# Decay sums of a gated delta rule: turned and spread by rounded products; the query norm folded into the output norm

## The reference, cut to what matters

```python
q = l2_normalize(q) * HEAD_DK ** -0.5          # after convolution and silu
k = l2_normalize(k)
g = jnp.cumsum(g_chunk)                        # log decay; exp(g_i - g_j) for j <= i
a_mat = strict * (k_beta @ k.T) * decay        # triangular system of a chunk, inverted
qk = lower * (q @ k.T) * decay
q_dec = q * jnp.exp(g)                         # meets the state: o = q_dec @ S + qk @ v_new
...
o = rms_norm_2(o_fwd + o_bwd, out_norm_g) * silu(z)
```

## Time and profile before

| | us |
|---|---|
| median of 3 runs | 1171.09 |
| lowest and highest run | 1166.39, 1172.75 |
| profiled execution: span from first to last instruction | 1167.6 |
| TensorE busy | 1019.9 (87%) |
| VectorE busy | 506.4 (43%) |
| ScalarE busy | 380.4 (33%) |
| GpSimd busy | 427.5 (37%) |

### The profile page before, as it was taken

The page is one execution under the profiler, slowest core; times in us unless marked ns, Lnnn a source line. Parts: engine busy times, 40 slices in busy tenths (PEclk is TensorE's granted clock), DMA queues, the critical chain, the costliest instruction groups (busy, mean ns, idle before and its releaser), DMA issues.

```text
span 1167.6 us, 20205 instructions
## 1 busy us (share of the span) xinstructions
PE 1019.9 (87%) x8173; PEld 802.9 (69%) x8173; DVE 506.4 (43%) x980; ACT 380.4 (33%) x572; POOL 427.5 (37%) x192
## 2 busy tenths in 40 slices
PE   8999999999999999999999899966767667666685
PEld 6999999999999999797989797423323232332231
DVE  4346965601136887767854543222222222222213
ACT  5554354444447656334343344100000000000002
POOL 6767868888876866143031281000000000000000
PEclk9999999999999999999999899988888888888898
DMA  7644546566656544215220889999999999999995
GB/s 248 219 129 146 178 129 187 175 192 186 183 178 196 165 146 137 59 37 217 93 80 12 326 293 383 388 425 428 429 427 428 429 427 429 428 428 429 428 420 202
DMA packets 43569, 304.75 MB, mean 261 GB/s; under 512 B 5092, under 2 KB 5476, under 8 KB 30952
## 3 DMA queue, kind: packets, MB, share of 16 engines
q1 hardware_dynamic: 43208, 303.21, 69.1%
q10 hardware_dynamic: 288, 0.52, 0.1%
HBM read 302.67 MB, written 1.05 MB: 260 GB/s over the span
## 4 chain that ended last, share of the span: by engine, by line
PE 57%; DMA 27%; DVE 8%; POOL 2%; issue 2%; ACT 2%; SPq 2%; DVEq 0%; ACTq 0%; POOLq 0%
DMA arena<-gate_up 24%; PE bank L484 11%; PE bank L485 11%; PE bank L486 10%; PE bank L1357 6%; PE bank L862 5%; PE bank L1378 3%; POOL rounded L2966 1%; DMA weights<-front 1%; DMA arena<-down 1%; PE bank L826 1%; DVE arena L2091 1%; POOL rounded L2925 1%; SPq L3010 1%; PE bank L1097 1%
## 5 line engine op out<-in xcount | busy, mean ns | idle before, releaser
L2925 POOL TENSOR_TENSOR rounded<-weights,rounded 128x1024 fp32r<-128x1024 f32 x152 | 370.4, 2463 | 156.3 <-ACT rounded L1443 146.9
L484 PE MATMUL bank<-rounded 128*128 128x256 f32 (+2 forms) x776 | 219.2, 282 | 2.2 <-POOL rounded L2925 2.2
L485 PE MATMUL bank<-rounded 128*128 128x256 f32 (+2 forms) x776 | 216.5, 279 | 0.0
L486 PE MATMUL bank<-rounded 128*128 128x256 f32 (+2 forms) x776 | 216.2, 279 | 0.0
L1443 ACT ACTIVATE rounded<-weights 128x1024 fp32r<-128x1024 f32 x146 | 147.4, 1052 | 80.6 <-PE bank L486 47.6
L484 PE MATMUL bank<-rounded,rounded 128*128 128x256 f32 (+3 forms) x552 | 158.3, 287 | 2.1 <-DVEq L2346 0.8
L485 PE MATMUL bank<-rounded,rounded 128*128 128x256 f32 (+3 forms) x552 | 156.2, 283 | 0.0
L486 PE MATMUL bank<-rounded,rounded 128*128 128x256 f32 (+3 forms) x552 | 156.1, 283 | 0.0
L484 PEld LDWEIGHTS bank<-rounded 128*128 128x128 f32 (+1 forms) x776 | 145.6, 188 | 4.3 <-POOL rounded L2925 2.9
L485 PEld LDWEIGHTS bank<-rounded 128*128 128x128 f32 (+1 forms) x776 | 145.5, 187 | 0.7 <-issue 0.6
L486 PEld LDWEIGHTS bank<-rounded 128*128 128x128 f32 (+1 forms) x776 | 145.2, 187 | 0.0
(11 more groups left out here) (465 smaller groups left out, 1456.6 us busy)
## 6 DMA issues: line engine op xcount, KB each, us to landing
weights<-front SPq DMA_DIRECT2D x165, 512.0 KB, 4.2
arena<-down SPq DMA_DIRECT2D x31, 2048.0 KB, 22.0
weights<-gate_up SPq DMA_DIRECT2D x28, 2048.0 KB, 34.7
arena<-gate_up SPq DMA_DIRECT2D x28, 2048.0 KB, 33.4
weights<-front SPq DMA_DIRECT2D x4, 2048.0 KB, 8.0
weights<-gate_up SPq DMA_DIRECT2D x8, 768.0 KB, 12.5
arena<-gate_up SPq DMA_DIRECT2D x4, 1536.0 KB, 33.7
weights<-gate_up SPq DMA_DIRECT2D x4, 512.0 KB, 7.3
```

What stands on the lines that cost most here:

```text
L484: nc.tensor.matmul(out, a[0], b[1], start=start, stop=False)
L485: nc.tensor.matmul(out, a[0], b[0], start=False, stop=False)
L486: return nc.tensor.matmul(out, a[1], b[0], start=False, stop=stop)
L2925: nc.gpsimd.tensor_tensor(lo, raw[q % RAW], hi.bitcast(f32), ALU.subtract).then_inc(sem("w_lo"), 1)
```

## The change

A unit is now two heads and both tiles. The decay sums of all heads are no longer formed by a product for each head: TensorE transposes the running sums `gsum` once (turn_rows), VectorE copies them as a rounded part and a rest (rows_r, partitions 0 to 15 and 32 to 47), and one rounded product of 48 rows with a picking column spreads a head's row of 256 tokens over all partitions. ScalarE makes the query exponentials from the same banks, directly after the exponentials of the unit, and it hands the banks back instead of VectorE. The decay sums in query_unit, the query factors, their spreading and the normalization of q are gone: as o is linear in q, the squared norm of q goes into the epsilon of the output norm (q_sums). `qd` and `inv` move to the end of the arena, where down weights arrive later; so two loads change places in SyncE's queue. `pairs` is formed between the convolutions of q0 and q1, GpSimd clears `inv` before its last four weight halves, and the substitution and query products are interleaved anew.

The diff, cut to its core (indentation reduced, unchanged lines left out):

```diff
@@ -290,12 +290,14 @@
 rn2_r = rounded(RING + top[0], LEN)
+q_sums = arena[:, top[0]:top[0] + SEQ]
...
-inv = place(32 * 32).rearrange("p (i j) -> p i j", i=32)
+inv_home = ARENA - BLOCK + 24 * P
+inv = arena[:, inv_home:inv_home + 32 * 32].rearrange("p (i j) -> p i j", i=32)
@@ -312,7 +314,11 @@
-qd = ring[2].rearrange("p (s c) -> p s c", s=LH)
+late_home = ARENA - BLOCK
+qd = arena[:, late_home:late_home + 24 * P].rearrange("p (s c) -> p s c", s=24)
+rows_r = rounded(RING + k_tok_at, 2 * P)
+pick_row_r = rounded(RING + k_tok_at + 2 * P, 16)
+ROW_SPREAD = 48
@@ -348,6 +354,14 @@
+def pair_lanes(x, d, u):
...
+    return x[:, 16 * d:16 * d + 16, :].rearrange("p (t h) c -> p t h c", t=TT)[:, :, 2 * u:2 * u + 2, :]
...
+def pair_of(bank):
...
+    return bank[:, :].rearrange("p (i t c) -> p t i c", i=2, t=TT)
@@ -967,21 +982,31 @@
             end(f, last)
...
+    def turn_rows():
...
+        f = begin("rows")
+        pe.wait_ge(sem("gl"), 4)
+        for t in range(TT):
+            last = nc.tensor.transpose(f.bank[0:16, t * P:(t + 1) * P], gsum[:, t + 1, 0:16], ident)
+        end(f, last)
...
-        tile, half = UNITS[u]
-        at = META + (tile - 1) * P
+        pe.wait_ge(sem("gl"), 5)
+        pe.wait_ge(sem("edec"), 1)
...
-            for h in range(4):
-                j = i * HEADS + 4 * half + h
-                last = nc.tensor.matmul(f.bank[:, h * P:(h + 1) * P], gl[:, tile, j:j + 1].to_broadcast([P, P]), omask(m),
+            for h in range(2):
+                j = i * HEADS + 2 * u + h
+                last = nc.tensor.matmul(f.bank[:, h * SEQ:(h + 1) * SEQ],
+                                        pick_row_r[0:ROW_SPREAD, j:j + 1].to_broadcast([ROW_SPREAD, P]), rows_r[0:ROW_SPREAD],
...
-        for h in range(4):
-            k = kT[:, 4 * half + h, at:at + P]
-            last = nc.tensor.matmul(f.bank[:, h * P:(h + 1) * P], k, k, start=True, stop=True)
+        for h in range(2):
+            for t in range(TT):
+                k = kT[:, 2 * u + h, META + t * P:META + (t + 1) * P]
+                last = nc.tensor.matmul(f.bank[:, (2 * h + t) * P:(2 * h + t + 1) * P], k, k, start=True, stop=True)
@@ -993,13 +1018,6 @@
         end(f, last)
-        for d, i, m in DIRS[0:1 if tile == TT else 2]:
-            f = begin(f"grow_{d}{u}")
-            for h in range(4):
-                j = i * HEADS + 4 * half + h
-                last = nc.tensor.matmul(f.bank[:, h * P:(h + 1) * P], gl[:, tile, j:j + 1].to_broadcast([P, P]), omask(m),
-                                        start=True, stop=True)
-            end(f, last)
@@ -1113,12 +1131,12 @@
     norms("nk", sq_k, LEN, ("sqn", 1, 2))
-    turn[WK] += 1
+    turn_rows()
...
@@ -1156,23 +1174,16 @@
     norms("nq", sq_q, SEQ, ("sqn", 3, 4))
+    query_unit(0)
...
+    query_unit(1)
...
-    spread("q", 0, 2, SEQ)
+    query_unit(2)
...
-    spread("q", 1, 2, SEQ)
-    turn[WK] += 1
-    z_part(4)
-    pe.wait_ge(sem("q_done"), 2)
-    query_unit(0)
-    z_part(5)
-    query_unit(1)
-    z_part(6)
-    query_unit(2)
-    z_part(7)
...
+    for n in range(4, 8): z_part(n)
@@ -1629,6 +1640,10 @@
         act.sem_inc(sem("gate_f"), 1)
...
+    act.wait_ge(sem("gl"), 1)
+    for a in (0, 32):
+        last = nc.scalar.activation(pick_row_r[a:a + 16, :], ident[a:a + 16, a:a + 16], ACT.Copy)
+    link(last)
@@ -1693,16 +1708,15 @@
             act.wait_ge(sem("unit_u"), 2 * u + i + 1)
-            e = qk[:, unit_lanes(i, u), :]
+            e = pair_lanes(qk, i, u)
...
-    def query_exps(u):
...
-        tile, half = UNITS[u]
-        for d, i, m in DIRS[0:1 if tile == TT else 2]:
-            f = got(f"grow_{d}{u}")
-            link(nc.scalar.activation(qd[:, unit_lanes(i, u), :], four_of(f.bank), ACT.Exp))
+        for d, i, m in DIRS:
+            f = fills[f"row_{d}{u}"]
+            if d == "f":
+                link(nc.scalar.activation(pair_lanes(qd, 0, u), pair_of(f.bank), ACT.Exp))
+            else:
+                link(nc.scalar.activation(qd[:, 16 + 2 * u:16 + 2 * u + 2, :], pair_of(f.bank)[:, 0], ACT.Exp))
@@ -1759,7 +1773,6 @@
     silu_sq("q", 1, qT[:, 4:8], SEQ, sq_q[:, 4:8])
-    norm_sqrt("nq", SEQ, ("ssn", 3), "sdn")
@@ -1767,11 +1780,7 @@
     take_gate("zz", 1)
-    query_exps(0)
-    query_exps(1)
...
-    query_exps(2)
-    query_exps(3)
@@ -2346,11 +2355,14 @@
         dve.sem_inc(sem(f"conv_{kind}"), 1)
...
-    def factors(name, n, rows_r, scale, signal, root, count):
+    def factors(name, n, rows_r, signal, root, count, of_queries=None):
...
-        link(nc.vector.tensor_scalar(rn, rn, scale, EPS, ALU.mult, ALU.add))
+        if of_queries is None:
+            link(nc.vector.tensor_scalar(rn, rn, 1.0, EPS, ALU.mult, ALU.add))
+        else:
+            link(nc.vector.scalar_tensor_tensor(rn, rn, 1.0 / P, of_queries, ALU.mult, ALU.add))
@@ -2367,6 +2379,8 @@
     link(nc.vector.memset(rn2_r.bitcast(f32), 0.0))
+    nc.vector.memset(rows_r.bitcast(f32), 0.0)
+    nc.vector.memset(pick_row_r.bitcast(f32), 0.0).then_inc(sem("gl"), 1)
@@ -2422,9 +2436,14 @@
         conv(f"v{h}", v_T[0][:, h, :], "v", 16 + h)
-    factors("nk", LEN, rn2_r, 1.0, "ssn", "sdn", 1)
+    factors("nk", LEN, rn2_r, "ssn", "sdn", 1)
...
+    f = got("rows")
+    link(nc.vector.tensor_copy(rows_r[0:16], f.bank[0:16, 0:SEQ]))
+    link(nc.vector.tensor_tensor(rows_r[32:48], f.bank[0:16, 0:SEQ], rows_r[0:16].bitcast(f32), ALU.subtract))
+    dve.sem_inc(free[f.b], 1)
+    dve.sem_inc(sem("gl"), 1)
@@ -2494,29 +2513,29 @@
     def unit_rows(u):
...
-        tile, half = UNITS[u]
...
-            e = qk[:, unit_lanes(i, u), :]
-            for h in range(4):
-                j = i * HEADS + 4 * half + h
-                last = nc.vector.scalar_tensor_tensor(e[:, h, :], f.bank[:, h * P:(h + 1) * P], gsum[:, tile, j:j + 1], amask(m),
-                                                      ALU.subtract, ALU.add)
+            e, row = pair_lanes(qk, i, u), pair_of(f.bank)
+            for t in range(TT):
+                for h in range(2):
+                    j = i * HEADS + 2 * u + h
+                    last = nc.vector.scalar_tensor_tensor(e[:, t, h, :], row[:, t, h, :], gsum[:, t + 1, j:j + 1], amask(m),
+                                                          ALU.subtract, ALU.add)
...
-            dve.sem_inc(free[f.b], 1)
...
-        tile, half = UNITS[u]
...
+        keys = pair_of(f.bank)
...
-            s = unit_lanes(i, u).start
-            for h in range(4):
-                j = i * HEADS + 4 * half + h
-                last = nc.vector.scalar_tensor_tensor(system[:, s + h, :], f.bank[:, h * P:(h + 1) * P], beta[:, tile, j:j + 1],
-                                                      qk[:, s + h, :], ALU.mult, ALU.mult)
+            s, e = pair_lanes(system, i, u), pair_lanes(qk, i, u)
+            for t in range(TT):
+                for h in range(2):
+                    j = i * HEADS + 2 * u + h
+                    last = nc.vector.scalar_tensor_tensor(s[:, t, h, :], keys[:, t, h, :], beta[:, t + 1, j:j + 1],
+                                                          e[:, t, h, :], ALU.mult, ALU.mult)
@@ -2623,24 +2642,26 @@
     dve.wait_ge(sem("to_tok"), 6)
-    for h in range(4):
+    conv("q0", qT[:, 0, :], "q", 0, META - 2, 2)
+    link(nc.vector.tensor_tensor(pairs, turned, turned.rearrange("p c r -> p r c"), ALU.add))
+    for h in range(1, 4):
...
-    link(nc.vector.tensor_tensor(pairs, turned, turned.rearrange("p c r -> p r c"), ALU.add))
...
-    factors("nq", SEQ, rn2_r, 1.0, "ssn", "sdn", 2)
...
-    substitute(0, 8)
-    normalize("q", 0, qT[:, 0:4], SEQ, P ** -0.5)
-    substitute(8, 11)
-    normalize("q", 1, qT[:, 4:8], SEQ, P ** -0.5)
-    substitute(11, 13)
+    substitute(0, 2)
+    f = got("nq")
+    link(nc.vector.tensor_scalar(q_sums[0:SUMS], f.bank[0:SUMS, 0:SEQ], EPS * P, EPS * EPS * P, ALU.mult, ALU.add))
+    dve.sem_inc(free[f.b], 1)
...
-    substitute(13, 18)
+    substitute(2, 9)
...
-    substitute(18, 23)
+    substitute(9, 14)
...
+    substitute(14, 19)
+    unit_queries(3)
+    substitute(19, 23)
@@ -2650,7 +2671,6 @@
         nc.vector.tensor_copy(system[q[i], lanes, q[i]], src[q[i], lanes, :])
-    unit_queries(3)
@@ -2702,7 +2722,7 @@
     link(nc.vector.memset(o_rn_r.bitcast(f32), 0.0))
-    factors("no", SEQ, o_rn_r, 1.0 / P, "ss_o", "sd_o", 1)
+    factors("no", SEQ, o_rn_r, "ss_o", "sd_o", 1, q_sums[0:SUMS])
@@ -2930,18 +2950,19 @@
                             pattern=[[0, NH], [1, P]], channel_multiplier=-1).then_inc(sem("ws_masked"), 1)
-    trail(range(WS_HALVES, N_HALVES))
...
-    for name in ("wf3", "q7"):
-        f = fills[name]
-        pool.wait_ge(full[f.b], f.n + 1)
-    nc.gpsimd.tensor_tensor(hn, hn_hi_r.bitcast(f32), hn_lo_r.bitcast(f32), ALU.add).then_inc(sem("hn"), 1)
+    trail(range(WS_HALVES, 2 * Q0))
...
+    trail(range(2 * Q0, N_HALVES))
...
+    for name in ("wf3", "q7"):
+        f = fills[name]
+        pool.wait_ge(full[f.b], f.n + 1)
```

(24 more changed lines are left out.)

## The result

The changed kernel takes 1175.49 us in the median (1174.86 to 1177.33) against 1171.09: the ratio is 1.0042, 95% interval 1.0030 to 1.0054. It is slower by 4.4 us, where 1 us faster was forecast; the time lies 1.0 us above the range. The profiled execution has a span of 1174.3 us, 6.7 more than the one before. That is more than the 4.4 of the medians, because the runs of one kernel differ: the execution profiled after took 1176.07 us, 0.6 over its median and 1.8 over its span; the one before, if 1.8 are added to its span too, was 1.7 under its own.

The account below looks back on a forecast made before the run. TensorE's own products were taken to bound the kernel until about 720 us, expert-weight transfers at the end. +1.35 +2.25 -6.30 +1.7 = -1.0 us, so 1170.1 us against the median; range 1164.0 to 1174.5 us.

Parts of the forecast that it names:

- (1): Key normalization: turning the sums and VectorE's row copies cost 0 to 0.2 us, taken as 0; memsets and two copies nothing.
- (5): Query convolutions: the moved sum of pairs delays q4 and the hn sum by 2.25 us; ends 1.54 and 2.84.
- (2): Units 0 and 1: ScalarE frees the row banks later, so Fourier products over tokens start about 0.3 us later.
- (3): Units 2 and 3: unit 2's first bank fills faster, giving VectorE a 0.7 us lead to unit 3's end.
- (4): Value transposes: bank 3 waits for ScalarE's extra exponentials, last transpose 1.35 us later; bounds 0.7 earlier, 2.1 later.
- (7): Wait before the last value transpose: TensorE's clock falls, Fourier output products lose 1.7 us; ends 0 and 2.8.
- rival B: Slower: the clock falls twice, at units 0 and 1 and before the values, 1174.0 us; chance 0.10.
- rule about transposes: Transposes don't count as clock activity as products do; one long fall before the values, 2.8 us, 1171.2 us; chance 0.08.
- A: Row savings arrive, the two late points (pairs, bank 3) don't: about -7.0 us, 1164.1 us; chance 0.18.
- C: Gain made, but the end is held by transfers issued early enough anyway: 1171.1 us; chance 0.09.
- D: Query stage: the inverse on VectorE is late, TensorE waits, -6.30 shrinks: 1170 to 1173 us; chance 0.05.
- (6): SP's queue: a gate_up and a down load swap places; GpSimd's clearing and query exponentials move; cost nothing.

Follow-up runs that it names:

- e1: The changed kernel with ScalarE's two 16x16 copies of the picking rows moved to just before the decay exponentials; 1169.2 us, ratio 0.9988 to the kernel before.
- e3: The kernel before with only the two 16x16 ScalarE copies added ahead of the first gate copies, result unused; 1177.2 us, ratio 1.0045 to the kernel before.
- e5: The changed kernel with GpSimd's second pair of pieces waiting until VectorE has formed the decays; 1168.7 us, ratio 0.9977 to the kernel before.
- e2: The changed kernel with ScalarE's two copies moved late and VectorE's two memsets moved behind the folds; 1168.5 us, ratio 0.9973 to the kernel before.
- e8: e2 with 14 and 16 discarded products filling TensorE's two waits at the value transposes; 1165.9 us, ratio 0.9957 to the kernel before.
- e7: e6 with each direction's query exponential taken by ScalarE ahead of that direction's own; 1166.0 us, ratio 0.9958 to the kernel before.
- e4: The changed kernel with the sum of pairs moved back behind conv q7; 1174.4 us, ratio 1.0022 to the kernel before.
- e6: e2 with the sum of pairs moved back behind conv q7; 1167.1 us, ratio 0.9959 to the kernel before.
- e9: The changed kernel with the moves of e2, e6, e7 and e8 together, 10 products in the second wait; 1163.3 us, ratio 0.9930 to the kernel before.

## Why the prediction was wrong

**The step that failed is the last sentence of (1):** the memsets and the "two 16x16 copies near 386 to 400 us lie beside other work, at most 0.5 us on engines that wait there anyway". It wasn't followed to who stands behind the copies: they hold up two roundings, these hold up GpSimd's pieces, and a gap of 0.68 us between pieces was what VectorE's small operations ran in. The row that showed it, 2.32 us for 16x16, stood in the earlier trace rows and was used for "pairs" in (5) alone. The cost was 8.2 us at the key norms instead of 0; e1, e3 and e5 show it from three sides. Without it the rest of the sum comes out within 1.1 us: e2 makes the change otherwise whole and stands 0.1 us behind the kernel before at the 32-blocks, where -1.0 was forecast. Its last value transpose is 2.4 us later than before (1.35 forecast; (1) and (2) below say why), the way from there to the hn sum is 4.0 longer (2.25 and 1.7 forecast), the query phase 6.31 shorter (6.30). That its median is 2.9 us under that of the kernel before is not in the sum: in the two profiles the way from the 32-blocks to the end is 575.8 us in e2 and 578.2 before, and why was not traced.

**(1), the rest.** The keys did come 1.6 us later than the norms account for; the stretch from 458.8 us has a clock of 0.60. With the norms restored, e1 and e2 keep 0.5 and 0.8 us, where 0 to 0.2 was forecast: TensorE waits there 0.3 and 0.6 us for VectorE's normalization, ahead of which VectorE now copies the rows.

**(2)** was right in its reason, and too small. In the changed kernel it doesn't show: no wait for ScalarE stands at units 0 to 2, and the first two units' rows take 0.82 and 0.65 us instead of 1.98. Of these 2.5 us 0.5 are left where the Fourier products over tokens begin (11.2 us from the keys, 11.7 before); between lies the clock of 0.60 from 469.0 us. But with the norms restored TensorE does wait for ScalarE's Fourier copies there. From e2, its waits at the keys and at these products:

```profile
PE bank L927 <- DVEq L2378: 0.6, 1, 0.6
PE bank L812 <- ACTq L1762: 0.8, 1, 0.8
```

e8 has the second wait too (0.8 us). In both the products begin 12.5 us from the keys, and 1.6 us later than before, where 0.3 was forecast. **(3)** VectorE started 0.47 us behind unit 2's rows, 1.13 before: a lead of 0.66, forecast 0.7.

**(4)** right in kind, the last transpose waits 3.1 us for ScalarE's second query exponential; e7 prices it at 1.3 us (1.35 forecast). **(5)** right: 2.3 by e4 and e6 (2.25); the operation took 2.11.

**The query phase** is right to 0.01 us: from the hn sum to the 32-blocks 55.41 before, 49.10 in e2 (49.11 in e8 and e9), -6.31 against -6.30. In the changed kernel 1.7 of it are lost to half speed in the first z part (5.40 for 3.72 us).

**(7)** was the right mechanism, and mis-sized by counting one fall: the fall before the values, here 496 to 503 us, was forecast at 1.7 us, and e8 shows 1.4 us for it up to the hn sum, but the granted clock fell at six other places from 384 to 560 us as well. The rival B, slower by two falls, named the mechanism. One fall came where it put it, at units 0 and 1 (0.60 from 469.0 us), but without the wait for ScalarE that was its reason, and the falls and waits from 404 to 425 us are not in it; so it is luck that its 1174.0 us lies only 1.5 under the median. On the rule about transposes (the Trainium skill, page "TensorE: Matmul & The Clock Gate", section "Part 4: PE-mode transpose"): the clock fell there in every run without fillers that has the change, which the rule would have too; no run puts transposes alone against products of the same length, so it stays open.

**A, C and D** didn't occur: the two late points came as (4) and (5) have it, the shift of 8.1 us at the 32-blocks is still 8.1 at 753 us, and the inverse was never waited for. 1.4 us are given back behind it, 0.6 of them by the end of the first gate_up transfer; where the rest goes was not traced. C misread a row: transfers stand at nine tenths from the 25th slice on (700 us), not from the 29th; nothing hangs on it.

**Open:** why the clock falls between 452 and 476 us in the runs e1 to e9 and not in the kernel before, whose waits for ScalarE at the spreading of the key factors are no shorter (1.06 and 0.40 us; 0.49 and 0.40 in e2). e3, with the code of before there, has it (0.54 from 465.6), so the new rows are not needed for it. The load swap of (6) was not tried by itself.

## What to carry to other kernels

An edit priced at nothing "beside other work" has to be followed through the queue behind it: here 0.45 us on ScalarE closed a gap on GpSimd that VectorE was living on, for 6 us. Where a trace shows a tiny VectorE operation as long as a GpSimd piece, count every such operation in reach of GpSimd's run, and order the two by a wait (e5: 6.7 us less than the changed kernel) rather than by luck. A new wait of TensorE can cost more than its length, by a stretch at the lower clock behind it; fill it or shorten it before adding up what the change saves. It need not: the waits of 1.5 and 1.4 us in the kernel before were followed by a granted clock of 1.00.

## What the runs showed of the hardware that was not expected

How sensitive it is: 0.45 us of unrelated work moved the key norms by 7.2 to 8.2 us, of which 4.7 to 4.8 are waits and the rest products at the lower clock. Also that 30 discarded products brought the 32-blocks 1.4 us forward (e8): with them in waits that TensorE had anyway its clock stayed at 1.00, where it read 0.50 without them.
